# The ple projection moved from the end of the third block into its first norm, its result kept in device memory

## The reference

```
h = rmsnorm(x, norm_g)                    # x: block 2's output, normalised by block 2's own final norm
proj = h @ w_in                           # split into xa, za, ub, gb, zb, gates
... the two branches give ya and yb ...
x = x + (sigmoid(g_a)*ya + sigmoid(g_b)*yb) @ w_out
ple_gate = sigmoid(rmsnorm(x, ple_norm_g) @ w_ple_gate)
x = x + (p @ w_ple) * ple_gate            # p: an input of 1024 x 256, w_ple: 256 x 1024
return rmsnorm(x, final_g)
```

## Time and profile before

| | us |
|---|---|
| median of 3 runs (lowest, highest) | 3979.28 (3974.26, 3979.71) |
| the profiled execution's own time | 3975.89 |
| its span, from the first to the last instruction | 3974.2 |
| PE busy | 3697.3 (93%) |
| DVE busy | 2166.8 (55%) |
| POOL busy | 1141.6 (29%) |
| ACT busy | 893.8 (22%) |
| mean granted TensorE clock | 0.966 of full |

### The profile page before, as it was taken

One profiled execution on the slowest core, in us unless ns is written; L12 is line 12 of the kernel. 1 busy time (PEld: TensorE's weight loads), 2 busy tenths in 40 slices (PEclk: granted clock), 3 DMA queues, 4 the chain that ended last, 5 costly groups with the idle time before them and its releaser, 6 DMA issues.

```text
span 3974.2 us, 44216 instructions
## 1 busy us (share of the span) xinstructions
PE 3697.3 (93%) x17330; PEld 2994.1 (75%) x17330; DVE 2166.8 (55%) x2115; ACT 893.8 (22%) x995; POOL 1141.6 (29%) x505
## 2 busy tenths in 40 slices
PE   7788999999999999998999999979999799989996
PEld 5677878877787887776788888866688688867875
DVE  7698541275843663545421221354289988866534
ACT  3344121121122331211210000112322122224221
POOL 0000433333333222223343443422122121123432
PEclk9989999999999998999999999998999899999998
DMA  3234313351136545533111111113334356664311
GB/s 127 74 80 121 95 42 116 111 169 43 37 127 147 160 137 140 144 93 111 43 47 48 47 48 48 46 23 112 130 120 139 111 158 172 167 209 152 98 51 53
DMA packets 536657, 407.18 MB, mean 102 GB/s; under 512 B 33192, under 2 KB 496424, under 8 KB 536512
## 3 DMA queue, kind: packets, MB, share of 16 engines
q1 hardware_dynamic: 476112, 289.74, 26.7%
q10 hardware_dynamic: 60400, 115.46, 7.8%
HBM read 286.81 MB, written 115.97 MB: 101 GB/s over the span
## 4 chain that ended last, share of the span: by engine, by line
PE 72%; DVE 16%; DVEq 4%; issue 3%; DMA 2%; ACT 2%; POOLq 1%; SPq 0%; POOL 0%; ACTq 0%
PE proj_ps L443 61%; DVE WORK L1112 5%; DVE Hlo L604 1%; DVE AUX L687 1%; PE mix_ps L1295 1%; PE mix_ps L2131 1%; PE mix_ps L2130 1%; ACT stage L471 1%; DVE Hlo L606 1%; PE mix_ps L708 1%; DVEq L685 1%; DVEq L550 1%; PE mix_ps L1442 1%; PE proj_ps L1453 1%; POOLq L413 1%
## 5 line engine op out<-in xcount | busy, mean ns | idle before, releaser
L443 PE MATMUL proj_ps<-Hhi,w_hi 128*128 128x512 f32 x4144 | 1329.1, 402 | 124.3 <-DVE Hlo L604 69.4
L443 PE MATMUL proj_ps<-Hlo,w_hi 128*128 128x512 f32 x4144 | 1289.3, 392 | 0.0
L443 PE MATMUL proj_ps<-Hhi,w_lo 128*128 128x512 f32 x4144 | 1286.7, 392 | 0.0
L411 POOL TENSOR_TENSOR w_hi<-w_raw,zero_col 128x1024 fp32r<-128x1024 f32 (+2 forms) x225 | 424.8, 1888 | 2200.9 <-PE proj_ps L443 1673.4
L443 PEld LDWEIGHTS proj_ps<-Hhi,w_hi 128*128 128x128 f32 x4144 | 772.3, 190 | 326.9 <-issue 89.0
L443 PEld LDWEIGHTS proj_ps<-Hlo,w_hi 128*128 128x128 f32 x4144 | 785.7, 190 | 168.7
L443 PEld LDWEIGHTS proj_ps<-Hhi,w_lo 128*128 128x128 f32 x4144 | 784.1, 189 | 167.5
L414 POOL TENSOR_TENSOR w_lo<-w_raw,w_hi 128x1024 fp32r<-128x1024 f32 (+2 forms) x225 | 579.1, 2574 | 32.0
L1112 DVE SCALAR_TENSOR_TENSOR WORK<-WORK,param_cols 128x1024 f32<-128x1024 f32 x240 | 369.1, 1538 | 18.8
L401 POOL TENSOR_TENSOR w_lo<-w_raw,w_hi 128x1024 fp32r<-128x1024 f32 x48 | 135.4, 2821 | 559.5 <-ACT w_hi L395 559.5
L471 ACT ACTIVATE stage<-proj_ps 128x1024 f32<-128x1024 f32 x104 | 122.0, 1173 | 620.8 <-PE proj_ps L443 619.9
(11 more groups left out here) (419 smaller groups left out, 3603.6 us busy)
## 6 DMA issues: line engine op xcount, KB each, us to landing
w_raw<-in_w_in SPq DMA_DIRECT2D x101, 512.0 KB, 4.5
w_raw<-in_sgu_w_in SPq DMA_DIRECT2D x24, 512.0 KB, 3.9
w_raw<-in_w_out SPq DMA_DIRECT2D x24, 512.0 KB, 4.3
w_raw<-in_w_gate SPq DMA_DIRECT2D x22, 512.0 KB, 3.9
w_raw<-in_w_up SPq DMA_DIRECT2D x22, 512.0 KB, 3.8
w_raw<-in_s_w_in SPq DMA_DIRECT2D x16, 512.0 KB, 4.2
WORK<-mid_acs SPq DMA_DIRECT2D x8, 1024.0 KB, 17.0
mid_qkv<-stage ACTq DMA_DIRECT2D x16, 512.0 KB, 5.2
```

The costliest lines, as they stand in the source:

```text
L411: nc.gpsimd.tensor_tensor(whi[slot][:, 0:kt, :], w, zero_col[:, 0:1].unsqueeze(2).to_broadcast([P, kt, P]), ALU.add)
L443: mm = nc.tensor.matmul(ps[:, h * HALF:(h + 1) * HALF], a[slot][:, k, :], b[:, k, h * HALF:(h + 1) * HALF], start=(k == 0 and n == 0), sto ...
```

## The change

The tiles of `ple` move from behind `ple_gate` to the merged norm `norm_g3`. The input p is loaded in two pieces into the last two slices of `WORK`'s first half, behind the first two weight loads of `down2`; it is split into slices 6 and 7 of `Hhi` and `Hlo` behind DVE's first addition of `down2` (`p_dve`, `p_act`). On PE, tiles 0 and 1 of `ple` stand ahead of the two sums, tile 2 between them and the spread, tiles 3 to 7 behind the spread and ahead of `xa`. ACT copies each tile out of PSUM into `stage` and stores it to a new buffer in device memory, with its copies between the splits of `norm_g3`. The splits of slices 6 and 7 wait for all tiles of `ple`. At the end, one DMA reads the whole result (8 x 512 KB) back into `WORK` in the place in SP's stream where p was loaded, and DVE does the product with the gate, the addition and the sum of squares of slice k-1 behind the eviction of gate tile k (`gated_add`), ACT the squares behind the sigmoids. The last gate tile is followed by `norm_last` alone.

```diff
-LAST_READER = dict(s5_gate=7, s5_glu=7, s5_out=7, sgu_gate=7, sgu_out=7, g=7, out_ssd=7, out_ret=7, gu2=11, zb=7, ya=7, yb=7, out3=7,
-                   ple_gate=7)
+LAST_READER = dict(s5_gate=7, s5_glu=7, s5_out=7, sgu_gate=7, sgu_out=7, g=7, out_ssd=7, out_ret=7, gu2=11, zb=7, ya=7, yb=7, out3=7)
...
+            self.hb["p"] = (self.h, 2, self.t)
+            self.h += 2
+            proj("ple", "w_ple_3", 0, 0, 8, "p", kt=2, store=True)
...
-            h("p", 2)
-            proj("ple", "w_ple_3", 0, 0, 8, "p", kt=2)
...
+            at = KT - 2 if p["src"] == "p" else 0
...
-                                              b[:, k, h * HALF:(h + 1) * HALF],
+                                              b[:, at + k, h * HALF:(h + 1) * HALF],
...
             for k in range(KT):
                 add_tile(dve, name, k // 2, k % 2)
                 dve.drain()
+                if k == 0 and norm == "norm_g3":
+                    p_dve(dve)
                 dve.wait_ge(S("sq_ready"), b["sq_ready"] + k + 1)
                 nc.vector.scalar_tensor_tensor(out=nrs, in0=nsq[1], scalar=mn_sq[:, k:k + 1], in1=nrs, op0=ALU.mult, op1=ALU.add)
                 nc.vector.tensor_tensor(nsq[0], nsq[0], nsq[1], ALU.add).then_inc(S("sq_added"), 1)
...
-        def add_gated(dve, name, norm, gate):
-
-            b = plan.nb[norm]
-            t0 = plan.p[name]["t0"]
-            dve.drain()
-            nc.vector.memset(nsq[0], 0.0).then_inc(S("sq_added"), 1)
-            for k in range(KT):
-                x, g = XT[:, k, :], gate[:, k, :]
-                dve.wait_ge(S("ple_gates"), k + 1)
-                dve.wait_ge(proj_done, t0 + k + 3)
-                nc.vector.tensor_tensor(g, g, PP[(t0 + k) % 2][:, :], ALU.mult).then_inc(psum_free, 1)
-                dve.drain()
-                nc.vector.tensor_tensor(x, x, g, ALU.add).then_inc(S("gated_added"), 1)
-                square_add(dve, b, k)
...
-            if k == KT - 1:
+            if k == KT - 1 or (name == "norm_g3" and k == KT - 2):
                 act.wait_ge(proj_done, tiles + 2)
...
-        def norm_merged_act(act, name):
+        def norm_merged_act(act, name, beside=None):
             b = plan.nb[name]
+
+            def store(m):
+                if beside and m < KT:
+                    store_tile(act, beside, m // 2, m % 2, ACT.Copy)
             with act.Fori(0, KT) as i:
                 square_act(act, b, i)
+            store(0)
+            store(1)
             rms_act(act, b, 0, mn_r, mn_eps)
             rms_act(act, b, 1, mn_sq, eps_rms[:, 0:1])
+            store(2)
             for k in range(KT):
                 split_hi(act, name, k, nhf[k % 2])
-
-        def norm_merged_pe(pe, name):
+                store(k + 3)
+
+        def norm_merged_pe(pe, name, beside=None):
             b = plan.nb[name]
+
+            def tiles(first, end):
+                for m in range(first, end if beside else first):
+                    pe_tile(pe, beside, m // 2, m % 2)
+            tiles(0, 2)
             sum_pe(pe, b, 0, nrs)
             sum_pe(pe, b, 1, nsq[0])
+            tiles(2, 3)
             spread_pe(pe, b, 0, nsq[1], SEQ)
+            tiles(3, KT)
...
         def norm_last_act(act, name):
             b = plan.nb[name]
-            with act.Fori(0, KT) as i:
-                square_act(act, b, i)
             rms_act(act, b, 0, mn_r, eps_rms[:, 0:1])
...
-        pl_T, pl_g = carve(2048, KT * SEQ)
-        pl_g = pl_g.rearrange("p (k n) -> p k n", k=KT)
+        pl_p, pl_g = carve(KT * SEQ, KT * SEQ)
+        pl_p, pl_g = (ap.rearrange("p (k n) -> p k n", k=KT) for ap in (pl_p, pl_g))
+        p_raw = [WORK[:, (KT - 2 + k) * SEQ:(KT - 1 + k) * SEQ] for k in range(2)]
+
+        def p_sync(sp):
+            for m in range(2):
+                load_tile(sp, "down2", 0, m)
+            sp.wait_ge(proj_done, plan.p["down2"]["t0"] + 2)
+            for k in range(2):
+                sp.dma_start(p_raw[k], t["p_turned"][k * P:(k + 1) * P, :]).then_inc(S("p_in"), 16)
+            project_load(sp, "down2", first=2)
+            project_load(sp, "ple")
...
+        def p_act(act):
+            for k in range(2):
+                act.wait_ge(hf_ready, plan.hb["p"][0] + k + 1)
+                nc.scalar.activation(Hhi[:, KT - 2 + k, :], p_raw[k], ACT.Copy).then_inc(hhi_ready, 1)
+
+        def p_dve(dve):
+            dve.wait_ge(S("p_in"), 32)
+            dve.drain().then_inc(hf_ready, 2)
+            for k in range(2):
+                dve.wait_ge(hhi_ready, plan.hb["p"][0] + k + 1)
+                nc.vector.tensor_tensor(Hlo[:, KT - 2 + k, :], p_raw[k], Hhi[:, KT - 2 + k, :].bitcast(F32), ALU.subtract)\
+                    .then_inc(h_ready, 1)
...
         def ple_sync(sp):
             sp.wait_ge(h_ready, plan.hb["merged"][0] + KT)
-            sp.dma_start(pl_T.rearrange("p (k n) -> p k n", k=2), t["p_turned"].rearrange("(k p) n -> p k n", p=P)).then_inc(S("p_in"), 16)
+            wait_stored(sp, "ple")
+            sp.dma_start(pl_p, tiles_of("ple")).then_inc(S("ple_in"), 16)
         def ple_gate_dve(dve):
+            b = plan.nb["final3"]
             t0 = plan.p["ple_gate"]["t0"]
-            for k in range(KT):
-                dve.wait_ge(proj_done, t0 + k + 3)
-                nc.vector.tensor_tensor(pl_g[:, k, :], PP[(t0 + k) % 2][:, :], nrs, ALU.mult).then_inc(psum_free, 1)
-                if k == KT - 2:
-                    ple_dve(dve)
+            for k in range(KT + 1):
+                if k < KT:
+                    dve.wait_ge(proj_done, t0 + k + 3)
+                    nc.vector.tensor_tensor(pl_g[:, k, :], PP[(t0 + k) % 2][:, :], nrs, ALU.mult).then_inc(psum_free, 1)
+                if k:
+                    gated_add(dve, b, k - 1)
+                else:
+                    nc.vector.memset(nsq[0], 0.0).then_inc(S("sq_added"), 1)
+                    dve.wait_ge(S("ple_in"), 16)
+
+        def gated_add(dve, b, k):
+            x, g = XT[:, k, :], pl_g[:, k, :]
+            dve.wait_ge(S("ple_gates"), k + 1)
+            nc.vector.tensor_tensor(g, g, pl_p[:, k, :], ALU.mult)
+            dve.drain()
+            nc.vector.tensor_tensor(x, x, g, ALU.add).then_inc(S("gated_added"), 1)
+            square_add(dve, b, k)
         def ple_gate_act(act):
-            for k in range(KT):
-                if k == KT - 1:
-                    ple_act(act, 0)
-                    ple_act(act, 1)
-                act.wait_ge(psum_free, plan.p["ple_gate"]["t0"] + k + 3)
-                nc.scalar.activation(pl_g[:, k, :], pl_g[:, k, :], ACT.Sigmoid).then_inc(S("ple_gates"), 1)
-
-        def ple_act(act, k):
-            split_hi(act, "p", k, pl_T[:, k * SEQ:(k + 1) * SEQ])
-
-        def ple_dve(dve):
-            dve.wait_ge(S("p_in"), 16)
-            dve.drain().then_inc(hf_ready, 2)
-            for k in range(2):
-                split_lo(dve, "p", k, pl_T[:, k * SEQ:(k + 1) * SEQ])
+            b = plan.nb["final3"]
+            for k in range(KT + 1):
+                if k < KT:
+                    act.wait_ge(psum_free, plan.p["ple_gate"]["t0"] + k + 3)
+                    nc.scalar.activation(pl_g[:, k, :], pl_g[:, k, :], ACT.Sigmoid).then_inc(S("ple_gates"), 1)
+                if k:
+                    square_act(act, b, k - 1)
...
-                project_load(sp, f"down{m}")
+                if m < 2:
+                    project_load(sp, f"down{m}")
+            p_sync(sp)
             block3_sync(sp)
             convb_sync(sp)
             project_load(sp, "out3")
...
             project_load(sp, "ple_gate")
-            project_load(sp, "ple")
...
+            norm_merged_pe(pe, "norm_g3", beside="ple")
...
             project_pe(pe, "ple_gate", first=2)
-            project_pe(pe, "ple")
...
-            norm_merged_act(act, "norm_g3")
+            p_act(act)
+            norm_merged_act(act, "norm_g3", beside="ple")
...
             ple_gate_dve(dve)
-            add_gated(dve, "ple", "final3", pl_g)
```

More of the change, by code:

```diff
@@ L2761, in _ @@
                 project_pe(pe, f"down{m}")
-            norm_merged_pe(pe, "norm_g3")
+            norm_merged_pe(pe, "norm_g3", beside="ple")
             mlstm_prep_pe(pe)
@@ L2861 @@
     "s5_branch", "s5_gate", "s5_ys", "sgu_v", "sgu_u", "sgu_gate", "sgu_y", "xbc2", "acs", "z", "qkv", "g", "ssd", "ret", "ug", "zb", "za",
-    "gg", "convb", "mlstm", "ya", "xs", "mlrows", "ml_q", "ml_k", "ml_v")}
+    "ple", "gg", "convb", "mlstm", "ya", "xs", "mlrows", "ml_q", "ml_k", "ml_v")}
 def kernel(**inputs):
```

## The result

| | median, us | runs |
|---|---|---|
| before | 3979.49 | 4, 3974.26 to 3982.36 |
| after | 3952.69 | 4, 3947.56 to 3959.72 |
| ratio | 0.9934 | 95% interval 0.992 to 0.9948 |
| predicted | 3953 | 3944 to 3963 |

The change makes the kernel 26.8 us faster by the medians. The profiled execution after is the longest of the four, 3959.72 (span 3958.0), 7.0 over their median. The one before, 3975.89 (span 3974.2), is not among its four runs and lies 3.6 under their median. So the two traces are 16.2 us apart and not 26.8. The two stretches that the change is about account for -24.2 of this; the rest, +8.0, lies ahead of them (4.7), between them (3.1) and behind them (0.2), where the work is the same in both. The experiments come back to it.

What follows compares the result with a forecast made beforehand. PE bounds the kernel up to the last gate tile, then a dependent loop with DVE and ACT. -31.7 + 1.6 + 6.1 = -24.0 us, giving 3951.9 from the profiled execution, 3955.3 from the median; forecast 3953, range 3944 to 3963.

Steps and rivals of the forecast that it cites:

- The end: Behind the last gate tile: six of eight gated additions go under gate tiles, final sum starts 31.7 us earlier.
- (a): Middle, from down2's end: ple tiles 0 and 1 fit in PE's idle time; cost nothing, 1.2 us to spare.
- (b): Merged norm: sums 5.0, tile 2 4.5, spread 2.7 us, together 12.2 against 10.63; +1.6 us, bounds -2.7 to +5.4.
- the sign that I named: At the merged norm: PE's granted clock falls inside the sums, near 2644.9, about 4.0 us after PE stops.
- (c): Behind the first spread: tiles 3 to 7, then xa's tile 0 after POOL's split; 28.1 against 22.0, +6.1 us.
- (d): Behind the spread: ACT's five copies and stores between its splits cost nothing; DVE's slices may take 22 us.
- Edits with no cost: p's load, copies and subtractions under down2 and the 4 MB read-back (15.8 us, slack 7) are all hidden.
- DVE held by the splits: Rival, 10%: POOL's five splits among the norm's slices delay DVE; -20.5 us in all, 3956.5.
- The dear middle: Rival, 11%: upper bounds of (b) and (c), +5.4 and +10.9; -15.4 us in all, 3961.5.
- the nearly free one: Rival, 12%: lower bounds of (b) and (c), -2.7 and +3.6; -30.8 us in all, 3946.2.
- The read-back is hidden: Before gate tile 0: the read-back delays nothing; the rival, 5%, had it up to 8 us late, -16, 3961.
- The serial tiles: Rival, 5%: behind the spread five ple tiles run in series, 7.95 us a step; +13.3 us in all, 3990.

Runs made afterwards that it cites:

- e3: The changed kernel with DVE's eight gated additions and ACT's squares all behind the last gate eviction; 3982.3 us, ratio 1.0013 to the kernel before.
- e12: The changed kernel unaltered, run again for a fourth profile; 3955.5 us, ratio 0.9938 to the kernel before.
- e8: The changed kernel unaltered, run again for a third profile; 3954.1 us, ratio 0.9939 to the kernel before.
- e1: The changed kernel unaltered, run again beside the first experiments; 3956.2 us, ratio 0.9938 to the kernel before.
- e5: The changed kernel with ple's new device-memory array listed last among the scratch arrays, no instruction differing; 3953.4 us, ratio 0.994 to the kernel before.
- e4: The changed kernel with ple's weights in two loads and two full-size splits of four tiles each; 3957.7 us, ratio 0.9943 to the kernel before.
- e7: As e4, but with ple's device-memory array listed last among the scratch arrays; 3953.2 us, ratio 0.9938 to the kernel before.
- e10: As e4, but POOL's second split of ple's weights waits for DVE's last sum of squares of down2; 3951.0 us, ratio 0.9923 to the kernel before.

## Why the prediction was right

**The end, -31.7.** Right. Measured 11.2 - 43.1 = -31.9, in each of four profiles of the changed kernel. Two additions behind the last one, as said; their pitch is 4.79 and not 4.97. e3 shows that the cover is what pays.

**(a), 0.** Right in its sum, with no time to spare where 1.2 us were forecast: tiles 0 and 1 are done at 2645.4, DVE's last addition ends at 2645.47, and the sums start at 2645.52.

**(b), +1.6.** The wrong sign: -0.4 in the first profile, -2.0 in e12 and e8 (15.3 us from down2's end to the first spread's end, against 17.3). Two terms were mis-sized. I left DVE's time to the sums as it was, 6.7 us; it is 5.4. In the kernel before, the split of xa's full-size weights stood beside DVE's last sum of squares, which took 2.99 us; it takes 1.28 now, and the split of ple's small weights (0.61 + 0.74 us, from 2640.16) is over before it starts; the next one, which starts 0.3 us behind it, takes 1.46 us where the others take 0.61. I had this split in the working of (a), but as a load on POOL, not as a hold on DVE, although I weighed that very hold for the slices. And the sums kept more of the full clock: 4.84 us in one profile and 3.7 in five others (e1, e3, e5, e8, e12), 5.0 predicted; tile 2 and the spread took 4.9 + 1.7 and 4.5 + 1.7, 7.2 predicted.

The reason that I gave for the clock's fall did not hold either. I counted 4.0 us from a stop of PE, and PE did not stop: it was busy for all 5.40 us ahead of the sums, at a clock of 1.00, and for all 11.50 behind, at 0.70 (the windows above). In the first profile the clock fell 2.3 us into the sums, whose matmuls have one column each, and was back at full 6.8 us later. In the five others it fell 0.4 to 0.9 us behind the sums, in tile 2, and for 3.4 us: in e12 it is 1.00 in 2641.5 to 2645.2, the sums, and 0.61 in 2645.2 to 2649.5. So the sign that I named, a fall inside the sums, came once in six profiles. What made it fall was not tested; an idle PE it was not.

**(c), +6.1.** Measured 30.2 - 22.0 = +8.2. The path was right step by step: POOL's w_lo of xa's tile 0 releases PE 17.5 us behind the spread, 17.2 predicted. The tile behind it was priced at full clock, 10.9; it took 12.73, since PE had stood for 3.6 us and some of its first pairs ran at 1.05 us (granted clock 0.50 in 2675.2 to 2678.5). In e4, e7 and e10, where the wait is 1.11 us, it takes 11.17. The term was mis-sized by the clock that a wait leaves behind it. The lower bound of (c), weights in time, is what the packed kernels reach: 25.8 us, 25.6 forecast.

**(d), 0.** Right: no row has PE waiting for ACT or for Hlo there. DVE's slices took longer than forecast, though: the last Hlo is written 24.6 us behind the spread (22 forecast, 20.3 before), and PE's first matmul of that slice starts at 28.8.

The middle in all is +7.7 in the first profile, as predicted, by two errors that cancel, and +6.1 in the others. With the end it makes -24.2 and -25.8; the ratios, 0.9934 to 0.9939, say -24 to -26 of 3979. That 3953 and 3952.69 lie 0.3 us apart is luck twice over: by those errors, and because the medians of four sets of runs of this kernel lie between 3952.7 and 3956.2.

**Edits with no cost.** Right. down2's tiles kept their 8.4 us. The read-back was issued at 3787.94, landed in 13.6 us (15.8 forecast), and POOL took the gate's first weights at 3815.35 with no wait for a transfer.

**The rivals.** DVE held by the splits: by the rule of "SBUF — State Buffer" in the Trainium skill (section "Who interferes with whom"), the splits should cost DVE time among the slices. They do: from the first spread to the second it is busy 24.4 us, before 20.8, and the pair e4 and e10 shows 3.10 against 1.29 us for one instruction beside and away from a full-size split. Beside it DVE ends 1.1 us behind POOL's split (2642.81 against 2641.73), as that rule has it. But PE never waited for it; the rival's other half fell. The dear middle and the nearly free one are both off by more than 5 us in the middle's own stretch (+16.3 and +0.9 against +6.1 to +7.7). The dear one's bound of (c) doesn't follow from its own terms: 28.1 + 4.0 + 2.7 is 34.8 and not 32.9, which would put that rival 1.9 us further off. The read-back is hidden. The serial tiles did not happen: five tiles in 13.87 us is PE's own pace.

**What I got wrong on the way.** I read a difference of 3.5 us between single profiles as a cost of the change, because it repeated in four of them. It took a second profile of the kernel before to see that it is scatter.

## What to carry to other kernels

When a dependent loop of DVE and ACT runs behind the last matmul, look for other work that can stand in front of it, so that the loop's steps lie under matmuls; what the moved work costs in its new place is the wait that its buffers and weight loads impose on the tile behind it, not its matmuls alone. A wait of PE of some us is to be priced with the slow matmuls that follow it. A second profile of the kernel before is worth as much as one of the kernel after: differences of a few us between single traces come and go.

## What was not expected of the hardware

- One stretch of the same program, 5,154 matmuls, took 1233.9 and 1237.4 us in two profiles of the kernel before, with 67 us of PE idle in each; PE's busy time moved by 3.7 us, and the granted clock was at half for 68.3 and 75.1 us.
- The granted clock fell while PE was busy without a gap, 2.3 us after its matmuls had gone from 512 columns to one (after), or 4.1 to 4.6 us after (e1, e3, e5, e8, e12).
- DVE's 128x1024 scalar_tensor_tensor on SBUF took 3.10 us with a 128x1024 split of POOL beside it and 1.29 without (e4, e10).
- Where one 4 MB array stands in the list of device-memory arrays went with PE's wait for a later weight load: 4.3 us with it last (e5, e7), 7.0 to 9.5 in the others; the time as a whole did not follow. Why was not tried.
